# Pooling head of a two-block decoder: weights loaded at once and scaled first, the sum of squares as one tree, and ten products of ones ahead of the projection

## The chip, the cores and the metric

One core of a Trainium2 chip runs the whole program. The metric is the device time of one execution in microseconds; the time before is the median of three executions. Engines are called by their names or by the short names of the profile: TensorE (PE, and PEld for its weight loads), VectorE (DVE), ScalarE (ACT), GpSimd (POOL) and SyncE (SP).

## What is computed

A sequence of 512 tokens with 1024 features goes through three layers: a pooling mixer with a gated feed-forward, windowed attention with a gated feed-forward, and a conformer convolution with a squared-ReLU feed-forward. The change touches the first layer's mixer alone:

```python
def pool_mixer(h, w, b, scale):          # h = rms_norm(x, norm_mix[0])
    csum = jnp.cumsum(hf, axis=1)
    for gi, win in enumerate((2, 4, 8, 16)):   # four groups of 256 features
        mean = (c - lo) / count[None, :, None]  # mean of the last `win` tokens
        outs.append(mean - hf[..., sl])
    y = jnp.einsum('bsgc,gcd->bsgd', p, w) + b
    return y.reshape(B, S, D) * scale
```

The mixer's result is added to x. The norm divides each token by the root of the mean of its squares over the 1024 features.

## The kernel before

**Layout.** Activations lie with features on the 128 partitions: `res` holds x as 8 tiles (c = 0 to 7) of 128 by 512 tokens. Tokens are cut into NBLK = 4 blocks of 128. The four pooling groups g own tiles 2g and 2g+1.

**Pooling head.** `project_pooled(g)` on TensorE multiplies raw x by the group's weights (scaled by the norm's gain g_mix0 into `wg`), 8 products 128x256 in two halves, each half ending in one bank of `acc` (chain n = 2g + half, `chain_done`). VectorE copies each half out in `evict_pooled(n)` into `zT`, which frees the bank (`acc_free`); chain n + 4 needs the bank of chain n. Then `window_mean(c)` multiplies `zT` by `mixed`, a matrix of window weights that is scaled by 1/rms of each token. So the norm is applied behind the projection, and its root is needed only for `mixed`.

**The root.** ScalarE squares the 8 tiles (`square(c)`, `squared`), VectorE adds them in pairs (`pair_squares(g)`, 4 sums, `pair_summed`), and TensorE adds over features and pairs in `token_sums(g)`: for each g 4 products of 128x4 with their 128x128 weight loads. Every float32 product has two records in the profile, so a projection of one g has 16 and the sums of one g have 8, 32 in all. They stand between the projections: 0, 1, sums 0 and 1, projection 2, sums 2 and 3, projection 3. ScalarE then takes the root (`rms4`), VectorE the reciprocal, and both write `mixed` (L932, L1319).

**The window weights.** GpSimd copies the identity out of `cst` and makes four shifted sums `near` (L420, L423). VectorE makes `mix` out of them in `window_weights()`, 20 small instructions. In VectorE's program its place is ahead of `evict_pooled(0)`.

**Loads.** ScalarE's queue issues, in this order, a head of `vec`, x tiles 0 to 3 in two transfers (`x_in[0]`, `x_in[1]`), `cst`, x tiles 4 to 7 in two transfers (`x_in[2]`, `x_in[3]`) and the rest of `vec`. SyncE's queue issues the weights in order of use: 4 pooling units (one 256 KB transfer each), of which unit k > 0 waits for `x_in[k]`, and then units of 512 KB into the same 4 slots of `raw`. Unit 4 waits for `lo_done` 1, that is, for VectorE's scaling of pooling weight 0, and so on.

**Weight scaling.** `weigh_pooled(g)` is half on ScalarE (L920, waits for the load) and half on VectorE (L1283, waits for ScalarE's half). In both engines' programs it stands between other work of the head, as the diff shows.

**Behind the head** the feed-forward of layer 1 starts: its first products need the tiles `xh` and `xl` of the new `res`, made by ScalarE and VectorE in turn (`prepare`), and weights split into `whi` and `wlo` (`split_hi`, `split_lo`). From there on three products for each weight tile follow each other on TensorE (L475 to L477).

Of the kernel before, what the change touches and what calls it, by code (L numbers as in the profile page):

```python
# [24 lines left out]
ALU = mybir.AluOpType  # L25
# [23 lines left out]
KT = 8  # L49
MASKED = -1.0e30  # L50
OVERLAY = 17584
MIX_STEPS = 16


# [95 lines left out]
def build(nc, xT, vec_in, cst_in, w_in, out):  # L150
# [3 lines left out]
    with ExitStack() as ctx:  # L154
# [3 lines left out]
        def sem(name):  # L158
            return ctx.enter_context(nc.semaphore(name))
# [80 lines left out]
        sq_ready = sem("sq_ready")  # L240
        squared = sem("squared")
        pair_summed = sem("pair_summed")
        ssum_ready = sem("ssum_ready")
        norm_done = sem("norm_done")
        rms_ready = sem("rms_ready")
# [85 lines left out]
        def square_of(c):  # L331

            return sq[:, c] if c < 2 else tmp[:, c - 2] if c < 6 else gate[:, c - 6]
# [36 lines left out]
        @block.sync  # L370
        def _(sp):

            def load(p, i, k):
                unit = p.unit + SLOTS * i + k
                if isinstance(unit, int) and unit < SLOTS:
                    free, at = None, unit - p.unit
                elif isinstance(i, int):
                    free, at = unit - SLOTS + 1, SLOTS * i + k
                else:
                    free, at = sp.snap(unit - SLOTS + 1), sp.snap(SLOTS * i + k)  # L380
                if free is None and k:
                    sp.wait_ge(x_in[k], 16)
                src = p.weights[at] if isinstance(at, int) else \
                    p.weights[bass.ds(at, 1)].rearrange("o p n -> p (o n)")
                if free is not None:
                    sp.wait_ge(lo_done, free)
                sp.dma_start(raw[:, k, 0:p.tiles * P], src).then_inc(w_loaded[k], 16)

            def load_qkv(p, e):
                sp.wait_ge(lo_done, p.unit + e - SLOTS + 1)  # L390
                sp.dma_start(raw[:, e % SLOTS, :], p.weights[QKV_ORDER[e]]).then_inc(w_loaded[e % SLOTS], 16)

            def load_wo(p, e):

                kh, c = e // SLOTS, 2 * (e % SLOTS)
                sp.wait_ge(lo_done, p.unit + e - SLOTS + 1)
                sp.dma_start(raw[:, e % SLOTS, :].rearrange("p (c n) -> p c n", c=2),
                             p.weights[c:c + 2, :, 4 * kh * P:4 * (kh + 1) * P].rearrange("c p n -> p c n"))\
                    .then_inc(w_loaded[e % SLOTS], 16)

            for p in order:
                if p.name in ("qkv", "wo"):
                    for e in range(p.units):
                        (load_qkv if p.name == "qkv" else load_wo)(p, e)
                else:
                    run(sp, lambda i: [load(p, i, k) for k in range(SLOTS)], p.units // SLOTS)
            last = ph["mlp_down3"]
            for c in range(C):
                sp.wait_ge(acc_free, last.chain + c + 1)
                sp.dma_start(out[:, c, :], res[:, c, :]).then_inc(stored, 16)  # L410
            sp.wait_ge(stored, 16 * C)
# [3 lines left out]
        def _(pool):  # L415
# [11 lines left out]
            def add_squares(name):  # L427

                per = 2 if name == "ain" else 1
                for n in range(per * C):  # L430
                    which, buf = (n % 2, n % 2) if name == "ain" else (0, n % 2)
                    pool.wait_ge(sq_ready, SQ[name] + n + 1)
                    pool.wait_ge(ssum_ready, SS[name] + n + 1)
                    nc.gpsimd.tensor_tensor(ssum[:, which, :], ssum[:, which, :], sq[:, buf, :], ALU.add)\  # L434
                        .then_inc(ssum_ready, 1)

            add_squares("ffn0")
            add_squares("qkv")
            for s in range(len(STEPS)):
# [32 lines left out]
        def _(pe):  # L472
# [73 lines left out]
            def project_pooled(g):  # L546

                pe.wait_ge(x_in[g], 16)
                pe.wait_ge(lo_done, g + 1)
                for h in range(2):  # L550
                    n = 2 * g + h
                    if n >= 4:
                        pe.wait_ge(acc_free, n - 3)
                    for e in range(2):
                        b = 2 * h + e
                        for t in range(2):
                            mm = nc.tensor.matmul(acc[n % 4][:, e * 2 * P:(e + 1) * 2 * P],  # L557
                                                  res[:, 2 * g + t, b * P:(b + 1) * P], wg[:, g, t, :],
                                                  start=(t == 0), stop=(t == 1))
                    mm.then_inc(chain_done, 1)  # L560

            def token_sums(g):

                pe.wait_ge(pair_summed, g + 1)
                for b in range(NBLK):
                    mm = nc.tensor.matmul(norm[0][:, 0:NBLK], square_of(2 * g)[:, b * P:(b + 1) * P], pick[:, b, :],
                                          start=(g == 0 and b == 0), stop=(g == 3 and b == NBLK - 1))
                if g == 3:
                    mm.then_inc(sqsum_done, 1)

            def window_mean(c):

# [12 lines left out]
                mm.then_inc(mean_ready, 1)  # L585

            pe.wait_ge(setup, 1)
            project_pooled(0)
            project_pooled(1)
            token_sums(0)  # L590
            token_sums(1)
            project_pooled(2)
            token_sums(2)
            token_sums(3)
            project_pooled(3)
            pe.wait_ge(mixed_act, 2)
            pe.wait_ge(mixed_dve, 2)
# [192 lines left out]
        def _(act):  # L790
# [120 lines left out]
            def square(c):  # L911

                if c % 2 == 0:
                    act.wait_ge(x_in[c // 2], 16)
                nc.scalar.activation(square_of(c), res[:, c, :], ACT.Square).then_inc(squared, 1)

            def weigh_pooled(g):

                act.wait_ge(w_loaded[g], 16)
                nc.scalar.activation(wg[:, g, 0, :].rearrange("p (o n) -> p o n", o=2),  # L920
                                     raw[:, g, 0:4 * P].rearrange("p (o t n) -> p o t n", o=2, t=2)[:, :, 0, :],
                                     ACT.Copy, scale=v("g_mix0", 2 * g)).then_inc(hi_done, 1)
# [9 lines left out]
                nc.scalar.activation(mixed[:, b], mix[:, 1 if b == 0 else 0], ACT.Copy, scale=rinv4[:, b:b + 1])\  # L932
                    .then_inc(mixed_act, 1)

            for g in range(4):
                square(2 * g)
                square(2 * g + 1)
                weigh_pooled(g)
                if g >= 2:
                    bias_residual(2 * g - 4)  # L940
                    bias_residual(2 * g - 3)
            act.wait_ge(sqsum_done, 1)
            nc.scalar.activation(rms4[:], norm[0][:, 0:NBLK], ACT.Sqrt, scale=1.0 / D, bias=eps[:, 0:1])\
                .then_inc(rms_ready, 1)
# [183 lines left out]
        def _(dve):  # L1128
# [198 lines left out]

            weigh_pooled(0)
            weigh_pooled(1)
            pair_squares(0)  # L1330
            pair_squares(1)
            window_weights()
            weigh_pooled(2)
            evict_pooled(0)
            evict_pooled(1)
            pair_squares(2)
            weigh_pooled(3)
            pair_squares(3)
            evict_pooled(2)
            evict_pooled(3)  # L1340
            dve.wait_ge(rms_ready, 1)
# [318 lines left out]
```

## Time and profile before

| | us |
|---|---|
| median of three runs | 1498.51 |
| lowest and highest | 1497.73 and 1498.73 |
| profiled execution, its own time | 1498.34 |
| span of its trace | 1496.2 |
| outside the span | 2.1 |
| TensorE busy | 1463.8 |
| first product of the trace | starts at 7.95 |

The span is what lies between the first and the last instruction. All times inside the trace are counted from the span's start. The granted clock of TensorE is given as a share of its full 2.4 GHz; 0.5 is the lower level, 1.2 GHz.

### The profile page before, as it was taken

How to read it: one execution, taken by the hardware profiler on the slowest of the kernel's cores; microseconds unless marked ns; L12 is line 12 of the kernel's file. 1: busy time of each engine (PE TensorE's matmuls, PEld its weight loads, DVE VectorE, ACT ScalarE, POOL GpSimd, SP SyncE). 2: the span in 40 equal slices, each digit the busy share in tenths (PEclk: the TensorE clock that was granted, in tenths of full speed). 3: DMA queues.
4: the chain of work that ended last, by engine and by line, in shares of the span. 5: the costliest groups of instructions: out<-in, count | busy, mean ns of one | idle time of the engine just before them, and what ended most of it. 6: DMA issues, size and time to landing. Idle time of an engine off the chain costs nothing.

```text
span 1496.2 us, 20225 instructions
## 1 busy us (share of the span) xinstructions
PE 1463.8 (98%) x6878; PEld 1204.8 (81%) x6878; DVE 941.7 (63%) x1350; ACT 655.3 (44%) x1064; POOL 215.7 (14%) x155
## 2 busy tenths in 40 slices
PE   7999999999999999999999999999779999999999
PEld 7888888888877898888888887777558888888887
DVE  6877774573555667767735735898888763544532
ACT  5444441341546664444413415888754322222210
POOL 1200000000302241000000006498612000000000
PEclk9999999999999999999999999999989999999999
DMA  5222223232322012332332323111112322232321
GB/s 185 71 98 99 98 98 113 76 107 74 123 92 65 29 58 85 99 101 95 99 113 80 104 72 109 57 57 57 39 45 100 113 98 99 91 106 84 105 99 49
DMA packets 38956, 132.45 MB, mean 89 GB/s; under 512 B 4208, under 2 KB 4464, under 8 KB 38896
## 3 DMA queue, kind: packets, MB, share of 16 engines
q1 hardware_dynamic: 37888, 128.99, 26.2%
q10 hardware_dynamic: 1008, 2.69, 0.5%
q8 instruction: 35, 0.57, 0.2%
q14 instruction: 25, 0.20, 0.0%
HBM read 129.56 MB, written 2.10 MB: 88 GB/s over the span
## 4 chain that ended last, share of the span: by engine, by line
PE 85%; POOL 7%; ACT 4%; DVE 2%; issue 1%; ACTq 0%; POOLq 0%; DVEq 0%
PE bank L475 27%; PE bank L476 26%; PE bank L477 26%; POOL prod L462 5%; POOL ssum L434 2%; PE bank L557 1%; PE bank L618 1%; PE bank L646 1%; PE bank L631 1%; ACT dgl L1061 1%; ACT dgh L1059 1%; PE bank L580 1%; DVE bank L1488 1%; ACT whi L799 0%; ACT tapped L1074 0%
## 5 line engine op out<-in xcount | busy, mean ns | idle before, releaser
L475 PE MATMUL bank<-xh,whi 128*128 128x512 f32 x1184 | 465.9, 394 | 1.4 <-DVE res L1423 0.7
L477 PE MATMUL bank<-xh,wlo 128*128 128x512 f32 x1184 | 460.8, 389 | 0.0
L476 PE MATMUL bank<-xl,whi 128*128 128x512 f32 x1184 | 460.7, 389 | 0.0
L799 ACT ACTIVATE whi<-raw 128x1024 fp32r<-128x1024 f32 x244 | 255.7, 1050 | 232.6 <-PE bank L477 232.5
L1137 DVE TENSOR_TENSOR wlo<-raw,whi 128x1024 fp32r<-128x1024 f32 x244 | 305.4, 1252 | 57.0 <-ACT whi L799 49.4
L475 PEld LDWEIGHTS bank<-xh,whi 128*128 128x128 f32 x1184 | 222.3, 188 | 50.8 <-issue 3.1
L476 PEld LDWEIGHTS bank<-xl,whi 128*128 128x128 f32 x1184 | 222.3, 188 | 48.0 <-issue 2.4
L477 PEld LDWEIGHTS bank<-xh,wlo 128*128 128x128 f32 x1184 | 222.3, 188 | 46.4
L475 PE MATMUL bank<-ahi,whi 128*128 128x512 f32 x608 | 236.5, 389 | 0.0
L476 PE MATMUL bank<-alo,whi 128*128 128x512 f32 x608 | 236.5, 389 | 0.0
L477 PE MATMUL bank<-ahi,wlo 128*128 128x512 f32 x608 | 236.5, 389 | 0.0
L1158 DVE TENSOR_TENSOR res<-bank,res 128x512 f32 (+1 forms) x80 | 55.3, 691 | 201.5 <-PE bank L477 201.5
L434 POOL TENSOR_TENSOR ssum<-ssum,sq 128x512 f32<-128x512 f32 x40 | 62.4, 1561 | 759.4 <-ACT sq L818 418.8
L1208 DVE SCALAR_TENSOR_TENSOR tmp<-u,vec,tmp 128x512 f32<-128x512 f32 x176 | 124.2, 748 | 29.0 <-ACT tmp L856 28.9
L477 PEld LDWEIGHTS bank<-ahi,wlo 128*128 128x128 f32 x608 | 114.1, 188 | 23.8
L475 PEld LDWEIGHTS bank<-ahi,whi 128*128 128x128 f32 x608 | 114.1, 188 | 23.7
L476 PEld LDWEIGHTS bank<-alo,whi 128*128 128x128 f32 x608 | 114.1, 188 | 23.6
L856 ACT ACTIVATE tmp<-u,vec 128x512 f32<-128x512 f32 x88 | 71.7, 815 | 126.8 <-DVE u L1203 126.7
L1203 DVE TENSOR_TENSOR u<-bank,rinv 128x512 f32<-128x512 f32 x88 | 59.7, 686 | 68.4 <-PE bank L477 68.4
L462 POOL TENSOR_TENSOR prod<-prod,tapped 128x512 f32<-128x512 f32 x65 | 99.2, 1526 | 18.6 <-ACT tapped L1074 9.7
L878 ACT ACTIVATE ahi<-tmp 128x512 f32 (+1 forms) x32 | 20.2, 632 | 121.9 <-DVE tmp L1233 121.9
L860 ACT ACTIVATE gate<-tmp 128x512 f32<-128x512 f32 x44 | 27.9, 634 | 96.3 <-DVE tmp L1208 96.3
(175 smaller groups left out, 1439.2 us busy)
## 6 DMA issues: line engine op xcount, KB each, us to landing
raw<-w_ffn_up SPq DMA_DIRECT2D x88, 512.0 KB, 3.3
raw<-w_ffn_down SPq DMA_DIRECT2D x32, 512.0 KB, 3.3
raw<-w_mlp_up SPq DMA_DIRECT2D x32, 512.0 KB, 3.3
raw<-w_mlp_down SPq DMA_DIRECT2D x32, 512.0 KB, 3.3
raw<-w_ain SPq DMA_DIRECT2D x16, 512.0 KB, 3.3
raw<-w_ffn_down SPq DMA_DIRECT2D x16, 384.0 KB, 3.0
raw<-w_qkv SPq DMA_DIRECT2D x12, 512.0 KB, 3.2
raw<-w_wo SPq DMA_DIRECT2D x8, 512.0 KB, 3.3
```

The lines of the kernel that those rows point to most:

```text
L434: nc.gpsimd.tensor_tensor(ssum[:, which, :], ssum[:, which, :], sq[:, buf, :], ALU.add)\
L462: nc.gpsimd.tensor_tensor(prod[:, c % 2, :], a, tapped[:, (made + k) % PARTS, :], ALU.add)\
L475: nc.tensor.matmul(out_, hi, mh, start=first, stop=False)
L476: nc.tensor.matmul(out_, hi, ml, start=False, stop=False)
L477: return nc.tensor.matmul(out_, lo, mh, start=False, stop=last)
L799: nc.scalar.activation(whi[:, s, 0:tiles * P], raw[:, s, 0:tiles * P], ACT.Copy)\
L856: nc.scalar.activation(tmp[:, k, :], u[:, k, 2:2 + T], ACT.Identity, scale=col(vec, par + 2), bias=col(vec, par + 3))\
L860: nc.scalar.activation(gate[:, b, :], tmp[:, 2 * b + 1, :], ACT.Silu)\
L1137: V.tensor_tensor(wlo[:, s, 0:tiles * P], raw[:, s, 0:tiles * P], whi[:, s, 0:tiles * P].bitcast(F32), ALU.subtract).then_inc(lo_done, 1)
L1158: V.tensor_tensor(row(res, c), acc[k][:], row(res, c), ALU.add).then_inc(acc_free, 1)
L1203: V.tensor_tensor(u[:, k, 2:2 + T], acc[k][:], rinv[:], ALU.mult).then_inc(acc_free, 1)
L1208: V.scalar_tensor_tensor(tmp[:, k, :], u[:, k, shift:shift + T], col(vec, par + 4 * j + shift), tmp[:, k, :], op0=ALU.mult, op1=ALU.add).t ...
```

## The change

The four pooling weights are issued without waiting for x. Both engines scale them at the head of their programs. GpSimd adds the squares of tiles 0 to 3 as a tree of three sums, behind `near`; VectorE adds those of tiles 4 to 7 as a tree of three. TensorE reads the two results once, behind projection 2: 8 products of 128x4 in place of 16. Ahead of the projection TensorE does ten products of a 128x128 tile of ones with itself into a bank that nobody reads.

```diff
+WARM = 10
@@ SyncE, load()
-                if free is None and k:
-                    sp.wait_ge(x_in[k], 16)
@@ GpSimd, behind near and ahead of add_squares("ffn0")
+            for g in range(2):
+                pool.wait_ge(squared, 2 * g + 2)
+                nc.gpsimd.tensor_tensor(square_of(2 * g), square_of(2 * g), square_of(2 * g + 1), ALU.add)\
+                    .then_inc(quad_steps, 1)
+            pool.wait_ge(quad_steps, 2)
+            nc.gpsimd.tensor_tensor(square_of(0), square_of(0), square_of(2), ALU.add).then_inc(quad_summed, 1)
@@ TensorE
-            def token_sums(g):
-                pe.wait_ge(pair_summed, g + 1)
-                for b in range(NBLK):
-                    mm = nc.tensor.matmul(norm[0][:, 0:NBLK], square_of(2 * g)[:, b * P:(b + 1) * P], pick[:, b, :],
-                                          start=(g == 0 and b == 0), stop=(g == 3 and b == NBLK - 1))
-                if g == 3:
-                    mm.then_inc(sqsum_done, 1)
+            def token_sums():
+                pe.wait_ge(pair_summed, 3)
+                pe.wait_ge(quad_summed, 1)
+                for g in (0, 2):
+                    for b in range(NBLK):
+                        mm = nc.tensor.matmul(norm[0][:, 0:NBLK], square_of(2 * g)[:, b * P:(b + 1) * P],
+                                              pick[:, b, :], start=(g == 0 and b == 0),
+                                              stop=(g == 2 and b == NBLK - 1))
+                mm.then_inc(sqsum_done, 1)
             pe.wait_ge(setup, 1)
+            for _ in range(WARM):
+                nc.tensor.matmul(bank[7][:, 0:P], ones[:], ones[:], start=True, stop=True)
             project_pooled(0)
             project_pooled(1)
-            token_sums(0)
-            token_sums(1)
             project_pooled(2)
-            token_sums(2)
-            token_sums(3)
+            token_sums()
             project_pooled(3)
@@ ScalarE
-            for g in range(4):
-                square(2 * g)
-                square(2 * g + 1)
-                weigh_pooled(g)
-                if g >= 2:
-                    bias_residual(2 * g - 4)
-                    bias_residual(2 * g - 3)
+            weigh_pooled(0)
+            square(0)
+            square(1)
+            weigh_pooled(1)
+            square(2)
+            square(3)
+            weigh_pooled(2)
+            weigh_pooled(3)
+            for c in range(4, C):
+                square(c)
+            for c in range(4):
+                bias_residual(c)
@@ VectorE
             weigh_pooled(0)
             weigh_pooled(1)
-            pair_squares(0)
-            pair_squares(1)
+            weigh_pooled(2)
+            weigh_pooled(3)
             window_weights()
-            weigh_pooled(2)
             evict_pooled(0)
             evict_pooled(1)
             pair_squares(2)
-            weigh_pooled(3)
             pair_squares(3)
+            dve.wait_ge(pair_summed, 2)
+            V.tensor_tensor(square_of(4), square_of(4), square_of(6), ALU.add).then_inc(pair_summed, 1)
             evict_pooled(2)
             evict_pooled(3)
```

## Rows read from the trace of the kernel before

**Rows 1.** Page, parts 1 and 4: busy time of engines; chain that ended last.

```profile
PE 1463.8 (98%) x6878; PEld 1204.8 (81%) x6878; DVE 941.7 (63%) x1350; ACT 655.3 (44%) x1064; POOL 215.7 (14%) x155
...
PE 85%; POOL 7%; ACT 4%; DVE 2%; issue 1%; ACTq 0%; POOLq 0%; DVEq 0%
```

**Rows 2.** Chain of work, 0 to 80 us: start us, length us, engine, line.

```profile
7.95 9.66 PE bank L557 x32
17.61 1.68 PE bank L566 x16
19.29 3.56 PE bank L557 x16
...
24.53 3.56 PE bank L557 x16
28.09 0.45 PE bank L580 x4
```

**Rows 3.** PE by itself, near 10 us: start us, length us, engine, line, operation.

```profile
9.36 1.06 PE L557 MATMUL bank<-wg,res 128*128 128x256 f32 x2
```

**Rows 4.** Timeline of all engines, first 27 us: VectorE, ScalarE, GpSimd and SyncE's queue.

```profile
1.97 0.08 DVE L1264 MEMSET pick<- 128x1 f32 x4
...
5.87 1.15 ACT L915 ACTIVATE sq<-res 128x512 f32<-128x512 f32 x2
6.92 0.49 ACT L920 ACTIVATE wg<-raw,vec 128x256 f32<-128x256 f32 x1
7.45 0.35 DVE L1283 TENSOR_SCALAR wg<-raw,vec 128x256 f32<-128x256 f32 x1 [2.55 <-ACT wg L920]
7.88 1.15 ACT L915 ACTIVATE tmp<-res 128x512 f32<-128x512 f32 x2 [0.46 <-DMA res<-xT]
...
8.54 0.29 POOL L420 COPY near<-cst 128x128 f32<-128x128 f32 x1 [8.09 <-DMA cst<-cst_in]
8.91 2.00 POOL L423 TENSOR_TENSOR near<-near 128x144 f32<-128x144 f32 x4
11.68 25.35 SPq L387 DMA_DIRECT2D raw<-w_ffn_up  x7
...
14.39 0.96 DVE L1304 SCALAR_TENSOR_TENSOR mix<-near 128x144 f32<-128x144 f32 x4
...
16.56 0.35 DVE L1283 TENSOR_SCALAR wg<-raw,vec 128x256 f32<-128x256 f32 x1
16.82 1.28 DVE L1297 COPY zT<-bank 128x512 f32<-128x512 f32 x2
...
25.68 1.43 ACT L932 ACTIVATE mixed<-mix,rinv 128x576 f32<-128x576 f32 x2
```

**Rows 5.** PE by windows: window, length, busy (instructions), granted clock, DMA share, GB/s.

```profile
5.00:8.00 3.00, 0.05 (x1) 1.00 1.02 345
...
1081.00:1085.00 4.00, 2.36 (x4) 0.55 0.37 119
1085.00:1088.00 3.00, 3.00 (x4) 0.50 0.04 16
...
1100.00:1105.00 5.00, 5.00 (x19) 0.81 0.01 3
```

**Rows 6.** PE around 1080 and 1099 us: idle time before an instruction in brackets.

```profile
1079.92 1.13 PE L751 MATMUL bank<-hv,ones 128*128 128x512 f32 x2 [1.39 <-DVE hv L1507]
...
1098.68 0.77 PE L475 MATMUL bank<-yhi,whi 128*128 128x512 f32 x1 [7.22 <-DVE ylo L1570]
```

**Rows 7.** VectorE beside GpSimd: timelines; line L1533 with ns min/median/max.

```profile
36.46 1.75 DVE L1144 SCALAR_TENSOR_TENSOR xl<-res,vec,xh 128x512 fp32r<-128x512 f32 x1
...
38.79 0.74 DVE L1144 SCALAR_TENSOR_TENSOR xl<-res,vec,xh 128x512 fp32r<-128x512 f32 x1
...
32.70 1.32 POOL L434 TENSOR_TENSOR ssum<-ssum,sq 128x512 f32<-128x512 f32 x1 [21.80 <-ACT sq L818]
...
L1533 DVE SCALAR_TENSOR_TENSOR hc<-tmp,vec,gate x8: 747/1268/1792, 947.8 to 1065.3; 128x512 f32<-128x512 f32 x8
```

More of the change, by code:

```diff
@@ L242, in build @@
         pair_summed = sem("pair_summed")
+        quad_summed = sem("quad_summed")
+        quad_steps = sem("quad_steps")
         ssum_ready = sem("ssum_ready")
```

## The prediction

> **What bounds the kernel now.** I read the page first: TensorE is busy for 98% of the span and carries 85% of the chain that ended last [rows 1]. So a change in the pooling head is worth what it moves TensorE's first product of the feed-forward; behind that point products follow each other, and an offset is carried to the end. Next comes the chain of work of the head, for where TensorE's time goes there. It starts its first product at 7.95 us, needs 9.66 us for projections 0 and 1 (32 records), 1.68 for token sums 0 and 1, 3.56 for projection 2, 1.68 again, 3.56 for projection 3, and starts the window means at 28.09 [rows 2]. It never waits between 7.95 and 28.09. Sixteen records take 3.56 us (0.222 each) in projection 2, so 32 should take 7.12, not 9.66. TensorE by itself shows why: near 10 us the records start 0.43 us apart (two, each 0.63 long, fill 1.06) [rows 3]. That is twice 0.222, the spacing of 1.2 GHz, although the granted clock reads 1.00 there; that column says nothing about the head. The excess of 2.54 us at 0.205 for each record is 12 slow records: slow until about 13 us, 4.9 us behind the first product. Last I read the timeline of the other engines for what will be late when TensorE is early [rows 4].
>
> **The change part by part: one number carries the sum.** It is S, the time at which projection 2 starts, now 19.29. Token sums: before, 16 products are 32 records of 0.105 us (16 in 1.68 [rows 2]), half of them ahead of S and half behind it. After, 8 products are 16 records, 1.68 us, all behind S. So behind S nothing changes (3.56 + 1.68 + 3.56), the 1.68 us ahead of it goes, and the gain at the window means is 19.29 - S.
>
> **Part 1, start of the projection.** ScalarE now squares two tiles from 5.87 and scales weight 0 at 6.92; VectorE's half starts 0.53 later and the product 0.50 after that [rows 4]. With the weight first, at 5.87, the product starts at 6.90. Its tile of x must have landed: it had by 5.87, but three more weight transfers (0.75 MB) now run beside it, and the DMA engines are full there (share 1.02, 345 GB/s) [rows 5]. Shared evenly, the 0.6 MB of x and vec ahead of it take up to 1.7 us more, so 6.9 to 7.6; I take 7.1. Later tiles and `cst` may come up to 0.75/0.345 = 2.2 us later.
>
> **Part 2, the ten products of ones.** They may start when `pick` is set, at 2.1 [rows 4]. They are 20 records of 128 columns; the window means have such records 0.11 apart (0.45 for 4) [rows 2], at the lower clock twice that, so 2.2 to 4.5 us, ending at 4.5 to 6.7, ahead of 7.1 and costing nothing. What they buy is the clock. The clock rose 4.9 us behind the first product in the head, and 3.2 us behind the one at 1098.68 (a share of 0.81 in 1100 to 1105 means 1.9 us at 0.5, so until 1101.9) [rows 5, 6]. Counted from 2.1 that is 5.3 to 7.0. I take the clock as full when the projection starts, so projections 0 and 1 take 7.12 and TensorE could begin projection 2 at 14.2. If it is not, they take 9.66 and it is 16.8.
>
> **Part 3, what is late next.** Projection 2 needs the bank that `evict_pooled(0)` frees, and on VectorE this stands behind `window_weights`, which stands behind GpSimd's `near` and so behind `cst`. Before, `near` was ready at 10.91, the window weights ran from 14.39 to 16.56, and TensorE was in projection 1 and the token sums all that time; the order cost nothing. That cover is what this change removes. Now: `cst` let GpSimd start at 8.54; bounds 8.5 to 10.7, and since the extra loads share the DMA engines with it for most of its way I take 9.9, so `near` is ready at 12.3 (2.37 later). Weights 2 and 3 need two more squares behind x_in[1], which came at 7.88 and may come up to 2.2 later: 7.9 plus 1.15 plus two halves 1.0 plus 0.5 gives 10.5, up to 12.7. So the window weights start at 10.9 to 12.9, I take 12.3. Alone they take 2.2; eviction 0 takes 0.64 and a hand-over: S from VectorE is 12.3 + 2.2 + 0.7 = 15.2, bounds 13.8 to 15.8, before the next term.
>
> **Part 4, the tree on GpSimd.** Its three sums follow `near` directly, so they run in exactly the stretch of the window weights. Alone one takes 1.32 [rows 7]. Beside such a sum a VectorE instruction with two operands in SBUF stretched from 0.74 to 1.75, and line L1533, which meets GpSimd's sums at varying phases, goes from 0.747 to 1.792 with a median of 1.268: 0 to 1.04 us of waiting, 0.52 in the middle [rows 7]. No row has twenty small instructions beside three sums. Lower bound 0, upper 3 by 1.32 = 4.0. VectorE always has an instruction queued here, so I expect nearly the largest wait at each sum, 3 by 0.9 = 2.7 (bounds of S with it: 13.8 to 19.8). S = 15.2 + 2.7 = 17.9, and 19.29 - 17.9 = 1.4 us of gain.
>
> The Trainium skill speaks to this. "SBUF — State Buffer", section "Who interferes with whom", says that a VectorE instruction with two SBUF inputs and a GpSimd one that reads SBUF exclude each other, the loser waiting for the whole of the other. By its rule each of the three sums would cost its full 1.32, so S would be 19.2 and the gain 0.1. The trace agrees in kind; its largest wait is 1.04 of 1.30.
>
> **Part 5, what the wait does to the clock.** TensorE would be idle from 14.2 to 17.9, 3.7 us. Behind idle times of 1.39 us (at 1079.92) and 7.22 us (at 1098.68) the granted clock was 0.5 [rows 5, 6]. The low level then costs half its length behind the restart: 3.2 us as at 1098.68 cost 1.6, 4.9 as in the head cost 2.4. I take 1.6. It eats the gain: 1.4 - 1.6 = -0.2.
>
> **Part 6, the rest.** The last sums of squares are no bound: GpSimd's tree ends near 12.3 + 4.0 = 16.3 or a little over, VectorE's behind eviction 1 at 18.5 plus 3 by 0.65 = 20.5; projection 2 ends at 21.5 at the earliest. The 512 KB loads, before issued from 11.68, come as early as 7.2 beside x; x_in[3] may land some 5 us later than before, near 16, and squares 6 and 7 are then done by 17.3. Behind the sums the order is as before: `mixed` is ready at 27.11, 1.0 us ahead of 28.09 [rows 2, 4], and keeps that distance. DMA issues of the four weights no longer wait on SyncE; nothing there was waited for except weight 1, which TensorE's slow start hid. Cost 0; if a later phase meets the clock at another moment, the low stretch of 1081 to 1088 (0.55 and 0.50) [rows 5] can change by a microsecond either way.
>
> **The sum.** Against the profiled execution (span 1496.2, 2.1 outside, 1498.34 in all): +0.2, so 1498.5; the median of the runs stands 0.17 above it, so 1498.7.
>
> **Rivals.**
> The cover holds: VectorE is hardly held up (0 to 1 us) because the small instructions slip between the sums. S = 15.2 to 16.2, gain 3.1 to 4.1; TensorE idles 1.0 to 2.0 us, and if the clock falls 1.6 is lost again. Centre without a fall 1498.5 - 3.6 = 1494.9, with one 1496.5. For: half of the waits of L1533 are below 0.52. Against: none can slip in while a sum holds the path. 0.28 together, evenly split.
> The products of ones do not do what they say: TensorE reaches projection 2 at 16.8, idles only 1.1, the clock stays. S = 17.9, gain 1.4, 1497.1. Also the result if the clock was up and stays up over the idle time. 0.17.
> Slower: VectorE blocked for each sum's whole time (S = 19.2, no gain) and the clock low for 4.9 to 6.7 us (1081.4 to 1088.1 by the windows [rows 5]), costing 2.4 to 3.35: 1500.9 to 1501.9. It turns the change into a loss once half of the low stretch is more than 19.29 - S. 0.12; only its upper third is over 0.2%. By the rule of the Trainium skill above, in "SBUF — State Buffer", this S is the one to expect.
>
> **How the numbers follow.** My forecast (S 17.2 to 18.7, low stretch 3 to 4.5 us: gain 2.1 to 0.6 less 1.5 to 2.25) gives 1497.9 to 1500.2, chance 0.43. 0.2% is 3.0 us, about what can be told from no change here. Faster than 1495.5 is the undisturbed half of the first rival, 0.14, and 0.02 of others: 0.16. Slower than 1501.5: 0.04. Within: 0.80. The range leaves out the better half of the undisturbed cover and the top of the slow rival: 1494.9 to 1500.9.
>
> **What would show each step.** Right: ones from 2.1, records 0.22 apart when the projection starts near 7.1; a wait of TensorE of 2 to 5 us for the first eviction ahead of projection 2; window weights of 4 to 6 us; records 0.43 apart behind it. Wrong: window weights of 2.2 to 3 us beside the sums, or `near` ready by 11, or no slow records behind the wait. The whole fails if another wait comes last at projection 2, or if the offset at the window means is not that at the end.

## The result, and the profile after

| | before | changed |
|---|---|---|
| median of 12 runs each, us | 1498.12 | 1501.33 |
| lowest and highest | 1496.98 and 1499.17 | 1500.3 and 1502.26 |
| span of the profiled execution | 1496.2 | 1499.0 |

The ratio is 1.0021, 95% interval 1.0013 to 1.0030: the change makes the kernel slower by 3.2 us. The forecast was 1498.7 in a range of 1494.9 to 1500.9, "no change".

The page, parts 1 and 4: the engines carry the same shares of the chain as in [rows 1].

```profile
PE 1467.0 (98%) x6882; PEld 1207.5 (81%) x6882; DVE 944.2 (63%) x1349; ACT 655.3 (44%) x1064; POOL 219.7 (15%) x158
...
PE 85%; POOL 7%; ACT 4%; DVE 2%; issue 1%; DMA 0%; ACTq 0%; POOLq 0%; DVEq 0%
```

The chain of work of the head, which answers to [rows 2] (start us, length us, what):

```profile
9.69 0.30 POOL near L421
...
12.10 4.16 DVE mix L1317 x4
...
17.54 0.61 DVE zT L1310
18.29 6.07 PE bank L564 x16
24.37 1.68 PE bank L575 x16
26.05 3.56 PE bank L564 x16
29.61 0.44 PE bank L589 x4
```

In the kernel before, this chain was TensorE's own from 7.95 on. Now it runs through the load of `cst`, GpSimd's `near`, VectorE's window weights and the first eviction, and only then reaches TensorE at 18.29. Projection 2 (x16) takes 6.07 us where it took 3.56, and the window means start at 29.61 instead of 28.09. The four instructions of line L1317, the first of the window weights, take 4.16 us, where the same four took 0.96 before [rows 4].

The timeline of the engines, which answers to [rows 4]; the bracket is the idle time ahead and what ended it:

```profile
2.11 4.36 PE L598 MATMUL bank<-ones 128*128 128x128 f32 x20 [2.11 <-DVE pick L1277]
...
6.78 7.14 PE L564 MATMUL bank<-wg,res 128*128 128x256 f32 x32 [0.30 <-DVE wg L1296]
...
12.02 1.26 POOL L440 TENSOR_TENSOR sq<-sq 128x512 f32<-128x512 f32 x1
12.10 4.16 DVE L1317 SCALAR_TENSOR_TENSOR mix<-near 128x144 f32<-128x144 f32 x4 [0.96 <-POOL near L424]
13.24 1.33 POOL L440 TENSOR_TENSOR tmp<-tmp 128x512 f32<-128x512 f32 x1
13.38 1.15 ACT L923 ACTIVATE gate<-res 128x512 f32<-128x512 f32 x2 [1.40 <-DMA res<-xT]
...
14.65 1.43 POOL L443 TENSOR_TENSOR sq<-sq,tmp 128x512 f32<-128x512 f32 x1
...
17.46 1.28 DVE L1310 COPY zT<-bank 128x512 f32<-128x512 f32 x2
...
18.29 6.07 PE L564 MATMUL bank<-wg,res 128*128 128x256 f32 x16 [4.37 <-DVE zT L1310]
```

The ten products of ones fill 2.11 to 6.47, and 32 records of the projection then take 7.14 us instead of 9.66. GpSimd's three sums (L440 twice, L443) run from 12.02 to 16.08, the same stretch as L1317. TensorE idles 4.37 us ahead of 18.29. The four instructions of L1317 by themselves (count, then shortest, median and longest in ns):

```profile
L1317 DVE SCALAR_TENSOR_TENSOR mix<-near x4: 294/1362/1372, 12.1 to 14.9; 128x144 f32<-128x144 f32 x4
```

Three of them are long and one is not: the first, second and fourth take 1.35 to 1.37 us, and the third, which starts at 14.67, just as GpSimd goes from its second sum to its third, takes 0.29.

The windows by granted clock show what stands behind this idle time (window, length, TensorE busy, granted clock, DMA share, GB/s):

```profile
18.30:24.40 6.10, 6.10 (x19) 0.61 0.00 0
24.40:29.40 5.00, 5.00 (x31) 1.00 0.02 5
```

A mean of 0.61 over 6.1 us is 4.8 us at half clock. It costs 2.4 us, and 6.07 - 3.56 is 2.5.

**The rest of the 3.2 us is 900 us further on.** Both kernels have the same wait near 936 us, TensorE for GpSimd's last sum of squares of the norm ahead of the convolution (`ain` in the kernel). Of the kernel before, then of the changed one (PE by itself, and the window around it with its granted clock):

```profile
935.70 1.98 PE L514 MATMUL bank<-ssum,ones 128*128 128x512 f32 x4 [2.42 <-POOL ssum L434]
...
935.00:940.00 5.00, 4.30 (x15) 1.00 0.26 94
```

```profile
937.18 3.11 PE L521 MATMUL bank<-ssum,ones 128*128 128x512 f32 x4 [2.39 <-POOL ssum L435]
...
937.00:942.00 5.00, 4.82 (x10) 0.66 0.28 105
```

Idle for 2.42 us before, 2.39 after, and 1.5 us later, which is the head's offset. But before, the clock stays at 1.00, and after, it is 0.66 over 5 us: 3.4 us at half clock, 1.7 us of cost. Three milestones further on (the first and the last start of the sums of L751, which is L759 after; the root of the last norm on ScalarE), of the kernel before and of the changed one:

```profile
L751 PE MATMUL bank<-hv,ones x16: 590/592/1090, 974.0 to 1082.1; 128*128 128x512 f32 x16
...
1153.06 0.69 ACT L822 ACTIVATE rms<-bank,eps 128x512 f32<-128x512 f32 x1 [2.79 <-PE bank L514]
```

```profile
L759 PE MATMUL bank<-hv,ones x16: 590/592/697, 977.1 to 1084.1; 128*128 128x512 f32 x16
...
1155.87 0.69 ACT L830 ACTIVATE rms<-bank,eps 128x512 f32<-128x512 f32 x1 [3.16 <-PE bank L521]
```

The offset is 1.5 us at 937, 3.1 at 974, 2.0 at the last of those sums (1082.1 against 1084.1), 2.8 at the last norm, and 2.8 at the end of the span. The medians are 3.2 us apart, 0.4 more than these two executions; single executions of one kernel differ by 2 us, so this rest is not followed up.

### The profile page after: what moved, and what is told of

It is laid out like the page before. It is cut to its first block, busy times and chain, and to the rows that moved or that the text cites. A ratio compares the mean times of both kernels' runs of the same rounds, so it can differ in the third digit from the quotient of the medians.

```text
span 1499.0 us, 20236 instructions
## 1 busy us (share of the span) xinstructions
PE 1467.0 (98%) x6882; PEld 1207.5 (81%) x6882; DVE 944.2 (63%) x1349; ACT 655.3 (44%) x1064; POOL 219.7 (15%) x158
## 4 chain that ended last, share of the span: by engine, by line
PE 85%; POOL 7%; ACT 4%; DVE 2%; issue 1%; DMA 0%; ACTq 0%; POOLq 0%; DVEq 0%
PE bank L482 27%; PE bank L483 26%; PE bank L484 26%; POOL prod L469 5%; POOL ssum L435 2%; PE bank L626 1%; ACT dgl L1074 1%; PE bank L654 1%; PE bank L639 1%; ACT dgh L1072 1%; ACT tapped L1087 1%; PE bank L564 1%; PE bank L589 1%; ACT whi L807 0%; DMA cst<-cst_in 0%
## 5 line engine op out<-in xcount | busy, mean ns | idle before, releaser
L868 ACT ACTIVATE gate<-tmp 128x512 f32<-128x512 f32 x44 | 27.9, 634 | 96.3 <-DVE tmp L1221 96.3
```

The lines of the kernel that those rows point to most:

```text
L868: nc.scalar.activation(gate[:, b, :], tmp[:, 2 * b + 1, :], ACT.Silu)\
```

## Experiments

All are compared with runs of the kernel before on the same chip. The changed kernel was not timed again beside them, so a difference to it is taken against the 1501.33 us above; the kernel before came out at 1497.66 to 1498.45 in the series below, so such a difference can be off by some 0.8 us. A trace shows one execution, and where that one lies far from the median, the text says so. In the timelines the window means start at 27.93 in the kernel before and at 29.44 in the changed one. Theory A says that the loss in the head is the eviction behind window weights that GpSimd's sums hold up, and the clock that falls in TensorE's wait. Its rivals: the extra loads (B, C), or something other than the clock behind the slow records. For the second loss, near 937, theory D says that it depends on the moment at which the old wait is met, and theory E that something in the change makes it.

### e1_evict_first: banks out ahead of the window weights

```diff
-            window_weights()
             evict_pooled(0)
             evict_pooled(1)
+            window_weights()
```

> The changed kernel, but VectorE copies out the first two banks ahead of the window weights. Theory A (the wait of 4.4 us ahead of projection 2 is that of the first eviction behind window weights that GpSimd's sums hold up, and it makes the clock fall): projection 2 starts at about 14 instead of 18.3, at full clock; the window weights still take 5 us (12.4 to 17.6), so the last pair sums end near 19.7 and TensorE waits about 2 us ahead of the token sums; window means start near 25 instead of 29.6, near 26.6 if the clock falls in that wait. Time 4.6 to 3 us below the changed kernel, 1496.7 to 1498.3. Theory B (projection 2 is late through something else, x or the loads): it still starts at 17 or later and the time stays near 1501.

Measured 1498.27 us against 1497.66 for the kernel before, ratio 1.0004 (0.9995 to 1.0013): no difference to it. Timeline:

```profile
6.62 10.60 PE L564 MATMUL bank<-wg,res 128*128 128x256 f32 x48
...
12.30 4.02 DVE L1317 SCALAR_TENSOR_TENSOR mix<-near 128x144 f32<-128x144 f32 x4
...
19.60 1.63 PE L575 MATMUL bank<-pick,sq 128*128 128x4 f32 x8 [2.38 <-DVE tmp L1351]
...
22.79 5.63 PE L564 MATMUL bank<-wg,res 128*128 128x256 f32 x16
...
28.26 0.61 PE L589 MATMUL bank<-mixed,zT 128*128 128x128 f32 x4
```

Projections 0 to 2 are one block of 48 records in 10.60 us. So neither x nor the loads hold up projection 2: theory B falls. The window weights still take 4.02 us for their first four instructions, the pair sums come late, and the wait has moved: 2.38 us ahead of the token sums, and the clock is low behind it. The token sums take 3.2 us instead of 1.7, and the 16 records after them 5.63 instead of 3.70, 3.4 us in all. The means start at 28.26; the expectation for a fall was 26.6.

### e2_tree_late: GpSimd's sums behind the window weights

```diff
+            pool.wait_ge(mix_steps, MIX_STEPS)
             for g in range(2):
                 pool.wait_ge(squared, 2 * g + 2)
```

> The changed kernel, but GpSimd's three sums wait until the window weights are made. Theory A: the window weights take 2.2 us instead of 5.4 (12.1 to 14.3), projection 2 starts at 15.0 to 15.3, TensorE idles 1.1 to 1.4 us ahead of it; the pair sums on VectorE now meet the sums on GpSimd and the token sums start at 19 to 20; window means near 24.5 to 26, time 1496.5 to 1498. Theory C (the late cst, by the loads issued at once, is the cause and the sums hold up nothing): window weights still take about 5 us, time near 1501.

Measured 1495.30 against 1497.66, ratio 0.9987 (0.9978 to 0.9996), below the 1496.5 to 1498 expected. Timeline:

```profile
12.08 0.96 DVE L1318 SCALAR_TENSOR_TENSOR mix<-near 128x144 f32<-128x144 f32 x4 [0.95 <-POOL near L424]
...
15.07 3.69 PE L565 MATMUL bank<-wg,res 128*128 128x256 f32 x16 [0.87 <-DVE zT L1311]
...
16.15 1.76 DVE L1304 TENSOR_TENSOR gate<-gate 128x512 f32<-128x512 f32 x1
...
19.63 1.06 PE L576 MATMUL bank<-pick,sq 128*128 128x4 f32 x8 [0.87 <-DVE tmp L1352]
...
24.98 0.61 PE L590 MATMUL bank<-mixed,zT 128*128 128x128 f32 x4
```

The four instructions take 0.96 us again, with `cst` and the loads as in the changed kernel: theory C falls, the sums are what stretched them. Projection 2 starts at 15.07. The sums now meet VectorE's pair sums instead, which go from 0.69 to 1.76 us (the second). TensorE waits twice for 0.87 us, and the clock stays full. One line is worth 6.0 us of the changed kernel's time. In the traces 4.5 us of it is the head (means at 24.98 instead of 29.44), of which 2.5 are the slow records that are gone; and the wait near 933 has no low stretch behind it here, which is 1.6 more (below). So more than half is what the clock does.

### e3_no_ones: without the ten products

```diff
-WARM = 10
+WARM = 0
```

> The changed kernel without the ten products of ones. Theory A: the clock then rises behind the projection's start instead of at 6.1, projections 0 and 1 take 9 us or more instead of 7.1 and end near 16, projection 2 still starts at 18.3 because the eviction is late; the idle time is 2 to 2.5 us instead of 4.4. If the clock falls all the same, the time stays at 1501; if it holds, window means start near 27.1, 2.5 us earlier, and the time is near 1498.7. A rival that the ones are what gains would put it 2 us above 1501.

Measured 1498.62 (1496.59 to 1502.66) against 1497.66, ratio 1.0006 (0.9997 to 1.0015). Timeline:

```profile
6.91 9.63 PE L564 MATMUL bank<-wg,res 128*128 128x256 f32 x32 [6.91 <-DMA res<-xT]
...
18.56 5.38 PE L564 MATMUL bank<-wg,res 128*128 128x256 f32 x16 [2.02 <-DVE zT L1310]
...
29.01 0.61 PE L589 MATMUL bank<-mixed,zT 128*128 128x128 f32 x4
```

Projection 2 starts at 18.56 without the ones and at 18.29 with them. In the changed kernel they mostly lengthen a wait (4.37 us instead of 2.02). Without them the median is 2.7 us lower, but the runs spread over 6 us. The trace is of one of the slow ones (1502.47), and in it the clock falls in a wait of 2.02 us too; that the fast ones are those in which it holds is likely, but no trace shows one.

### e4_both: e1 and e2 together

```diff
+            pool.wait_ge(mix_steps, MIX_STEPS)      # GpSimd, ahead of its sums
-            window_weights()                        # VectorE
             evict_pooled(0)
             evict_pooled(1)
+            window_weights()
```

> The changed kernel with both: the first two banks out ahead of the window weights, and GpSimd's sums behind them. Theory A: projection 2 starts at 14, the window weights run from 12.4 to 14.6, GpSimd's sums from 14.6 to 18.7 beside VectorE's pair sums, which end at 18 to 19.5; TensorE idles 1 to 2 us ahead of the token sums; window means start at 24 to 25, 1.6 more if the clock falls there. Time 1495.5 to 1497.5, below the kernel before.

Measured 1498.08 (1495.94 to 1501.01) against 1497.66, ratio 0.9998 (0.9989 to 1.0007): a miss. Timeline:

```profile
14.70 2.26 POOL L441 TENSOR_TENSOR sq<-sq 128x512 f32<-128x512 f32 x1 [2.51 <-DVE mix L1328]
...
18.71 1.26 POOL L444 TENSOR_TENSOR sq<-sq,tmp 128x512 f32<-128x512 f32 x1
...
20.11 1.84 PE L576 MATMUL bank<-pick,sq 128*128 128x4 f32 x8 [2.92 <-POOL sq L444]
...
23.52 6.71 PE L565 MATMUL bank<-wg,res 128*128 128x256 f32 x16
...
30.06 0.61 PE L590 MATMUL bank<-mixed,zT 128*128 128x128 f32 x4
```

With the eviction early, TensorE reaches the token sums at 17.2, but GpSimd's last sum runs until 19.97. The wait is one of 2.92 us instead of two of 0.87. The clock falls in it: the token sums take 3.4 us, and 16 records 6.71, which is 4.7 us more than at full clock. Two edits of which one left a wait of 2.38 us and the other two of 0.87 gave one of 2.92 together. This trace is of the slowest of the eleven executions (1501.01); whether the clock fell so long in the median one no trace shows.

### e5_filler: the wait of the changed kernel filled with products that do no work

```diff
             project_pooled(1)
+            for _ in range(18):
+                nc.tensor.matmul(bank[7][:, 0:P], ones[:], ones[:], start=True, stop=True)
             project_pooled(2)
```

> The changed kernel with 18 more products of ones (36 records of 0.11 us, 4.0 us) between projections 1 and 2, into a bank that nobody reads. They do no work; they only fill the 4.4 us in which TensorE waits for the first eviction. Theory A (half of the loss is the clock, which falls in that idle time): projection 2 still starts at 18.3, but takes 3.6 us instead of 6.1; window means start at 27.1 instead of 29.6; time 2.5 us below the changed kernel, near 1498.8. Rival (the slow records of projection 2 come from something else, such as VectorE or DMA beside them): projection 2 takes 6 us as before and the time is 1501 or more.

Measured 1498.98 against 1498.45, ratio 1.0002 (0.9993 to 1.0011), so 2.4 us below the changed kernel. Timeline:

```profile
18.47 3.69 PE L564 MATMUL bank<-wg,res 128*128 128x256 f32 x16 [0.23 <-DVE zT L1312]
...
27.23 0.61 PE L589 MATMUL bank<-mixed,zT 128*128 128x128 f32 x4
```

Projection 2 starts at 18.47, as late as before, but takes 3.69 us, and the means start at 27.23. The slow records were the clock's, and it fell because TensorE was idle. VectorE, GpSimd and the loads ran beside it all the same. The head gains 2.2 us by it (29.44 to 27.23). The wait near 937, met at 935.01, has no low stretch in this trace either; the execution traced took 1497.76, 1.2 us less than the median.

### e6_reordered: a head without waits

```diff
@@ GpSimd: its three sums ahead of near instead of behind it
@@ VectorE
-            window_weights()
             evict_pooled(0)
             evict_pooled(1)
             pair_squares(2)
+            evict_pooled(2)
+            evict_pooled(3)
             pair_squares(3)
             dve.wait_ge(pair_summed, 2)
             V.tensor_tensor(square_of(4), square_of(4), square_of(6), ALU.add).then_inc(pair_summed, 1)
-            evict_pooled(2)
-            evict_pooled(3)
+            window_weights()
```

> The changed kernel with a head in another order: GpSimd makes its three sums ahead of near (about 9.8 to 13.8), VectorE copies out banks 0 to 3 and makes its three sums ahead of the window weights. By theory A no wait of TensorE over 0.5 us is left: projection 2 starts at 13.9, token sums at 17.5, projection 3 ends at 22.7, where the window means start, 5.4 us ahead of the kernel before. The window weights are made at 16.3 to 18.5, before the root is there. Time 1492 to 1493.5. If TensorE waits over 1.5 us somewhere after all and the clock falls, 1.6 to 2.5 us more.

Measured 1493.79 against 1498.45, ratio 0.9964 (0.9950 to 0.9978): faster than both kernels, by 4.7 us and by 7.5, in five executions, and 0.3 us above the 1492 to 1493.5 expected. PE by itself:

```profile
6.69 10.60 PE L564 MATMUL bank<-wg,res 128*128 128x256 f32 x48
...
18.83 3.70 PE L564 MATMUL bank<-wg,res 128*128 128x256 f32 x16
```

Forty-eight records, the token sums and the last sixteen follow each other; the means start at 22.36, 5.6 us earlier than before. All parts of the change are in this kernel. They pay once GpSimd's sums no longer run beside the window weights, and the window weights, which nobody needs before the root, no longer stand ahead of the evictions. Of the 5.6 us, 4.7 are in the median; the trace has a low stretch at 931.5 and two of 10.2 us near 1075 and 1088.

### e7_before_ones and e8_before_loads: single parts, put into the kernel before

e7 puts the loop of ten products ahead of projection 0. e8 takes out the wait for x_in and puts the scaling first on both engines:

```diff
@@ e8: SyncE
-                if free is None and k:
-                    sp.wait_ge(x_in[k], 16)
@@ e8: VectorE; ScalarE as in the change
             weigh_pooled(0)
             weigh_pooled(1)
+            weigh_pooled(2)
+            weigh_pooled(3)
             pair_squares(0)
             pair_squares(1)
             window_weights()
-            weigh_pooled(2)
             evict_pooled(0)
             evict_pooled(1)
             pair_squares(2)
-            weigh_pooled(3)
             pair_squares(3)
```

> The kernel before with the ten products of ones alone. The clock is full from about 6; projection 0 takes 3.6 us from 7.95 and ends at 11.5, projection 1 then waits for weight 1, scaled at 13.3, 1.8 us; it ends at 16.9, the token sums at 18.5, window means at 27.3, 0.8 us earlier: 1497.0. If the clock falls in the 1.8 us: 1498.7 to 1499.5. The rival that ones cannot raise the clock for the projection gives the time of before, 1497.7, with the first records 0.43 apart.

> The kernel before with the loads at once and the weights scaled first alone: no ones, its four pair sums on VectorE and its token sums in two places. The projection starts at 6.8 to 6.9, the clock rises between 10 and 12, projection 1 ends at 15 to 16.5, the token sums at 16.6 to 18.2. Nothing on GpSimd holds up the window weights (2.2 us, ending near 14.8), so the first eviction is in time. Projection 2 starts at 16.6 to 18.2, 1.1 to 2.7 us earlier than before: 1495 to 1496.6. Theory C (late cst and x by the loads cost the gain): projection 2 starts at 19 or later and the time is that of before or more.

e7: 1498.33 against 1498.45, ratio 0.9998 (0.9989 to 1.0007), no difference, where 1497.0 was expected. e8: 1496.32 against 1498.45, ratio 0.9989 (0.9980 to 0.9998), 2.1 us faster by the medians. PE of e7, then of e8:

```profile
7.82 3.69 PE L557 MATMUL bank<-wg,res 128*128 128x256 f32 x16 [1.69 <-DVE wg L1285]
12.38 3.69 PE L557 MATMUL bank<-wg,res 128*128 128x256 f32 x16 [0.87 <-DVE wg L1285]
```

```profile
6.80 9.37 PE L555 MATMUL bank<-wg,res 128*128 128x256 f32 x32 [6.80 <-DVE wg L1286]
...
17.71 3.70 PE L555 MATMUL bank<-wg,res 128*128 128x256 f32 x16
```

In e7 the clock is full from the first record (3.69 us for 16). Weight 1 still comes late, and TensorE waits 0.87 us for its scaling. The means start at 26.39, 1.5 us earlier than before, and yet the median shows nothing of it. The trace is of the fastest of the eleven executions (1497.18), and in it 1.2 of the 1.5 us reach the end (span 1495.1 against 1496.2); where the others lost it no trace shows. In e8 the projection starts 1.2 us earlier and projection 2 at 17.7, with no sums on GpSimd beside the window weights. Of the two parts tried alone it is the one that paid, and its loads hold up nothing that matters. The shorter token sums alone were not tried.

### Four more traces: how steady are the low stretches?

> The changed kernel again, one look, for how its low clock stretches fall in another execution. Head: the wait of 4.4 us ahead of projection 2 and a low stretch behind it are there again, window means at 28.8 to 30.5. The second loss, the low stretch of 3.4 us at 938 behind the 2.4 us wait for GpSimd: theory D (it is a matter of the moment at which that same wait is met, as the kernel before had the wait of 2.42 us too) expects it in some executions and not in others; theory E (the change causes it each time) expects it in every one.

> The kernel before again, one look. Window means at 26.9 to 28.5, as the first records are slow for 3.4 to 5.5 us. Theory D expects the low stretch near 936 in some executions of this kernel too; theory E in none.

> The changed kernel a third time; the same expectations as for the second look: wait of 4.4 us and low clock in projection 2 each time, the low stretch near 938 by theory D in some looks, by theory E in each.

> The kernel before a third time; by theory D the low stretch near 936 appears in some of the looks at either kernel, by theory E in none of this one.

The times were 1501.25, 1498.28, 1501.46 and 1498.27. The changed kernel waited 4.53 and 4.15 us ahead of projection 2 and had slow records behind it both times; its window means started at 29.4 and 29.7, those of the kernel before at 26.9 and 27.9. The low stretch at 938 was there in all three traces of the changed kernel, and in none of three of the kernel before, though each met the wait of 2.4 us. Theory D had expected it in some executions of a kernel and not in others, which did not come; so far this speaks for theory E.

One pair of these traces shows more. The kernel before started its means at 26.93 in one execution and at 27.93 in another, met the wait 1.0 us earlier too (934.72 and 935.70), and both spans are 1496.2: an offset of 1.0 us was gone at the end, with no edit at all.

### d1_before_later and d2_after_later: the same wait, met later

```diff
@@ d1: the kernel before, 7 products; d2: the changed kernel, 9 products
             project_pooled(3)
+            for _ in range(7):
+                nc.tensor.matmul(bank[7][:, 0:P], ones[:], ones[:], start=True, stop=True)
             pe.wait_ge(mixed_act, 2)
```

> The kernel before with 7 products of ones (14 records, 1.55 us) between projection 3 and the window means: nothing else, it only comes 1.5 us later, as the changed kernel does. Theory D (the low stretch near 938 depends on the moment at which the 2.4 us wait is met, which the head shifts): the low stretch appears in this kernel too, and the time is 1498.1 + 1.5 + 1.6 = 1501.2. Theory E (something else in the change makes it): no low stretch there, 1499.6.

> The changed kernel with 9 products of ones (18 records, 2.0 us) at the same place. Theory D: the wait is met 2.0 us later still, at another moment against the low stretches, and the one near 938 vanishes: 1501.3 + 2.0 - 1.6 = 1501.7. Theory E: it stays, 1503.3.

d1: 1500.44 against 1498.03, ratio 1.0013 (1.0004 to 1.0022). d2: 1501.36 against 1498.03, ratio 1.0031 (1.0021 to 1.0041). PE at the wait, of d1 and then of d2:

```profile
936.61 2.87 PE L514 MATMUL bank<-ssum,ones 128*128 128x512 f32 x4 [2.40 <-POOL ssum L434]
```

```profile
938.07 1.98 PE L521 MATMUL bank<-ssum,ones 128*128 128x512 f32 x4 [2.39 <-POOL ssum L435]
```

Four records behind the wait take 1.98 us at full clock. In d1 they take 2.87: the kernel before, only later by 0.9 us at the wait (936.61 against 935.70), gets the low stretch that it did not have, and loses 2.4 us for 1.55 us of added work. In d2 they take 1.98: the changed kernel loses the stretch when it comes later still. Its median is that of the changed kernel in spite of 2.0 us of added work. But its runs spread (1499.89 to 1505.20), and the trace is of the fastest, in which the low stretch of the head was shorter as well (projection 2 in 5.21 us), so that it came only 0.9 us later than the changed kernel (938.07 against 937.18). What the median execution did near 938 no trace of d2 shows. Theory E falls by d1, which has nothing of the change in it and whose trace (1500.70) is near its median. (d1 is 0.8 us below its expected time, d2 0.3.)

All traces together say how good theory D is. They are sorted here by the moment at which TensorE resumes behind the wait, for the sixteen in which it was not filled; the last column is the time from there to the first of the convolution's sums (974.0 in the kernel before).

| TensorE resumes at, us | traces | clock behind the wait | to the first sum, us |
|---|---|---|---|
| 930.2 | e6 | low | 39.9 |
| 932.8 to 935.7 | e2, e7, e8, e5, e1, and all three of the kernel before | full | 38.3 |
| 936.6 to 937.6 | d1, e3, e4, and all three of the changed kernel | low | 39.9 to 40.0 |
| 938.1 | d2 | full | 38.3 |

The moments of the two kinds do not mix, whatever the kernel, and each low stretch costs the same 1.6 us. The first and the last row rest on one trace each.

### f3_after_fill and f5_reordered_fill: what the stretch near 938 is worth

```diff
                     if t == C - 2:
+                        for _ in range(8 if norm_name == "ain" else 0):
+                            nc.tensor.matmul(bank[7][:, 0:P], ones[:], ones[:], start=True, stop=True)
                         sum_features(norm_name)
```

> The changed kernel with 8 products of ones (16 records, 1.8 us) ahead of the norm's sum in which TensorE waits 2.4 us for GpSimd near 937. They lie inside the wait and move nothing. If the low stretch there is worth 1.6 us, it is gone and the time is 1499.7; if the loss is elsewhere, the time stays at 1501.3.

> The version with the head in another order and the same 8 products of ones near 930, where its look had a low stretch of 3.4 us too. Expected 1493.8 - 1.6 = 1492.2 by theory D; 1493.8 if its low stretch there was not in every execution.

f3: 1500.24 against 1498.03, ratio 1.0020 (1.0011 to 1.0029), 1.1 us below the changed kernel where 1.6 was expected. f5: 1493.85 against 1498.03, ratio 0.9971 (0.9960 to 0.9982), the same as e6 within the spread: a miss. PE of f3:

```profile
933.94 1.95 PE L505 MATMUL bank<-ones 128*128 128x128 f32 x16
936.50 1.98 PE L523 MATMUL bank<-ssum,ones 128*128 128x512 f32 x4 [0.61 <-POOL ssum L435]
```

The stretch is gone in both traces, and both then take 38.3 us to the first sum. In f5 the time did not follow. Its trace has low stretches of 10.2 us near 1075 and near 1088, at the end of the convolution, as e6 has. In this pair of traces the saving is lost in that part: f5 reaches the first sum 1.3 us ahead of e6 (968.8 against 970.1), but the last norm only 0.1 ahead (1148.70 against 1148.84). f3 keeps 1.3 of the 2.3 us by which it was ahead of the changed kernel at the first sum. Whether e6 also had the stretch near 930 in only some executions stays open.

## Why the prediction was wrong

**Right, with sizes.** The projection started at 6.78 (7.1 forecast). The ones raised the clock before it, and 32 records took 7.14 us (7.12). `near` was ready at 12.06 (12.3). The window weights ran beside GpSimd's three sums and took 5.4 us, 3.2 more than alone (2.7 forecast, within 0 and 4.0). Projection 2 waited for the first eviction and started at 18.29 (17.9). TensorE idled 4.4 us (3.7), and the clock was at its lower level behind it. The gain at S was 1.0 us (1.4). The token sums did not wait; the last x landed by 13.4, earlier than the 16 that I allowed for.

**The term that was mis-sized.** Part 5 priced the low clock behind the restart at 1.6 us, after the 3.2 us of 1098.68, with 2.4 as the other bound. It was 4.8 us low, 2.5 us lost. With this the head costs 1.5 us instead of 0.2. The two traces of the same kernel that followed agree (6.03 and 6.12 us for projection 2). In the traces of d2 and f3 it took 5.2 and 5.3 us, so 1.6 is also seen; the upper bound was met in three of these five.

**The step that failed.** Part 6 let an offset be carried to the end unchanged and allowed a microsecond either way near 1081. That is not how it went. The wait of 2.4 us near 937, which the prediction does not name, has full clock behind it in the kernel before; met 1.5 us later it has a low stretch behind it, and costs 1.6 us more. A loss in the head is not carried, it is changed: d1 lost 2.4 us for 1.55 of added work. The eighteen traces say where. From the window means to the wait near 937 all take 907.4 to 907.8 us, and from the last norm to the end 343.2; there an offset is carried. From the wait to the first sum of the convolution they take 38.3 or 39.9, and from there to the last norm, across the low stretches of the convolution's end, 178.3 to 180.5; what decides within that last range was not worked out.

In numbers of the profiled pair: +0.2 forecast, 0.4 for S, 0.9 for the clock behind it, 1.6 for the wait near 937, less 0.3 behind the first sum, is +2.8, and +3.2 in the medians. So the time lies 0.4 us above the range.

**The rivals.** "The cover holds" fell by 4.16 us against 0.96. "The ones do not do what they say" fell by the trace. The slow one had half of it: the clock was low for 4.8 us, more than twice the gain, and so the head became a loss. But it wanted S at 19.2 and no gain, and S was 18.3 with a gain of 1.0. That the measured 1501.3 lies in its 1500.9 to 1501.9 is luck: it needed the 1.3 us from behind the head, which this rival does not have. I gave it 0.12 and tied it to a fuller block than was needed. The rule of the Trainium skill ("SBUF — State Buffer", "Who interferes with whom") would have put S at 19.2. The trace agrees with its exclusion: each of the three long instructions ended 0.16 or 0.17 us behind the end of the sum that it met (13.45, 14.75 and 16.26 against 13.28, 14.58 and 16.09). The cost is below the whole of a sum, 3.2 us for three or 1.07 each against 1.26 to 1.43, since each sum had started 0.08 to 0.23 us before the instruction did. That lies between the rule's 1.32 and my 0.9, and S of 18.3 nearer to my 17.9 than to 19.2.

**The chances.** 0.80 for a change within 3.0 us and 0.04 for slower: the measured 3.2 us stands at that edge. The forecast itself leaned to the slow side by 0.2 us, and each large term that was off (S, the clock, the later wait) was off the same way. With the upper bound of the clock's price taken as likely as the lower, the slow side deserved, by my estimate, a quarter of the chances.

## What to carry to other kernels

Before work is put on GpSimd, look at what VectorE does with two operands in SBUF at that time and who waits for that; here three sums of 1.3 us held up three small instructions for 3.2 us, and an eviction behind them. A wait of TensorE costs its length and then, where the clock falls, another 1.6 to 4.7 us (in these traces), so compare orders by their longest wait, not by the sum of their waits: two of 0.87 us were cheap, and those of 2.0 to 4.4 us in the head were not. An offset of one or two microseconds early in a program can change what an unrelated wait costs later, so read where the clock was low in more than one trace before a difference of 0.1 to 0.2% is given to an edit.

## What the runs showed of the hardware

The same wait of 2.4 us near 930 to 938 was met in sixteen traces where it was not filled: three of the kernel before, three of the changed one, e1 to e8, d1 and d2. The clock was low behind it in seven (the three of the changed kernel, e3, e4, e6 and d1) and stayed up in nine. The length of the wait, 2.36 to 2.42 us, does not tell them apart; the moment does, as the table shows.

GpSimd's sums did not slow all twenty small instructions of the window weights. They held the first, the second and the fourth until the sum that each had met was over, one for each sum. The third slipped through at the change from the second sum to the third, in 0.29 us, its old pace, and the other sixteen ran behind the sums at theirs (16.18 to 17.55).

The granted clock reads 1.00 from the start of a trace, also where records are 0.43 us apart (near 10 us in the kernel before [rows 3]); only the spacing of records tells the clock there.
